# A hybrid decoder trunk on one core: gate rows between the first merge's rounds, the recurrent branch's halves interleaved, the first fox projection ahead of the merge

## The reference, cut to what matters

```python
def causal_depthwise_conv(x, w, b):           # 4 taps
    y = xp[:, 0:S] * w[0] + b
    for k in range(1, CONV_WIDTH):
        y = y + xp[:, k:k + S] * w[k]
...
def rg_lru(x, wa, ba, wx, bx, lam):           # x: the convolved input, 8 blocks of 128 channels
    r = sigmoid(blockdiag(x, wa) + ba)
    i = sigmoid(blockdiag(x, wx) + bx)
    log_a = -LRU_C * r * softplus(-lam)
    a, u = exp(log_a), sqrt(-expm1(2 * log_a)) * (i * x)
    h[t] = a[t] * h[t-1] + u[t]
...
# forgetting attention ("fox", 16 heads of 64) and mLSTM (8 heads of 128)
c = cumsum(log_sigmoid(f_logit))              # the gate rows: one row of 512 tokens for each head
merged = sum_b sigmoid(gate_b) * (y_b @ w_br_b)
x = x + merged @ w_out
x = x + PEER(rms_norm(x))                     # product-key experts
```

## Time and profile before

| | |
|---|---|
| median of 3 runs | 4959.5 us (4953.31 to 4968.77) |
| the profiled execution | 4969.86 us, span 4968.0 us |
| mean granted clock of PE | 0.954 |
| PE, DVE, ACT, POOL busy | 90%, 64%, 36%, 55% |
| layer 1, first full slot to the first fox step | 38.5 to 297.7 us |
| the same place in layer 2 | some 2475 us later |

### The profile page before, as it was taken

How to read it: one execution, slowest core, us unless ns; L and a number is a source line. 1 busy time by engine, 2 the same in 40 slices (tenths; PEclk the granted TensorE clock), 3 DMA queues, 4 the chain that set the end, 5 groups by cost and what they waited for, 6 DMA issues and landing times.

```text
span 4968.0 us, 73244 instructions
## 1 busy us (share of the span) xinstructions
PE 4472.6 (90%) x21194; PEld 3701.0 (74%) x21194; DVE 3170.9 (64%) x5031; ACT 1764.3 (36%) x3196; POOL 2725.2 (55%) x1477
## 2 busy tenths in 40 slices
PE   6899999889988887999978999998898888879998
PEld 4666775679888886777756667756798888867776
DVE  7434224448889775888884342243488897768888
ACT  2234213114555652333322341231145556523332
POOL 5643663555455665555456426636554566645554
PEclk8999999999999998999989999999999999989999
DMA  2211221124578999999712112212246799999996
GB/s 96 68 60 35 76 81 46 68 71 133 180 242 257 297 294 309 342 336 331 288 67 72 56 35 81 80 44 69 71 141 185 240 259 297 301 313 341 348 333 248
DMA packets 463132, 893.19 MB, mean 180 GB/s; under 512 B 41376, under 2 KB 320416, under 8 KB 459808
## 3 DMA queue, kind: packets, MB, share of 16 engines
q1 hardware_dynamic: 387424, 617.22, 38.3%
q0 software_dynamic: 73728, 268.47, 15.7%
q10 hardware_dynamic: 1728, 4.89, 0.3%
HBM read 787.65 MB, written 102.76 MB: 179 GB/s over the span
## 4 chain that ended last, share of the span: by engine, by line
PE 59%; DVE 16%; DMA 10%; issue 8%; ACT 4%; SPq 2%; DVEq 1%; POOL 1%; ACTq 0%; another core or an unknown queue 0%; POOLq 0%
DMA ring<-v_tab 6%; PE pair L749 6%; PE bank L749 6%; PE bank L1120 5%; PE bank L1125 5%; PE bank L1115 4%; PE bank L1063 4%; PE bank L775 3%; DMA ring<-u_tab 3%; PE pair L775 3%; PE pair L752 3%; PE bank L752 3%; PE bank L906 2%; PE bank L1094 2%; PE bank L1067 2%
## 5 line engine op out<-in xcount | busy, mean ns | idle before, releaser
L631 POOL TENSOR_TENSOR w_hi<-ring,ones 128x1024 fp32r<-128x1024 f32 x272 | 546.4, 2009 | 939.0 <-PE bank L775 276.5
L619 POOL TENSOR_TENSOR w_lo<-ring,w_hi 128x1024 fp32r<-128x1024 f32 x256 | 633.2, 2474 | 566.5 <-ACT w_hi L1408 559.7
L1063 PE MATMUL bank<-xT,w_hi 128*128 128x384 f32 x2048 | 729.8, 356 | 22.6 <-ACT gst L1420 18.9
L1063 PE MATMUL bank<-xl_peer,w_hi 128*128 128x384 f32 x2048 | 707.0, 345 | 0.4 <-issue 0.4
L634 POOL TENSOR_TENSOR w_lo<-ring,w_hi 128x1024 fp32r<-128x1024 f32 x272 | 690.1, 2537 | 21.3
L1414 ACT CAST w_hi<-ring 128x1024 fp32r<-128x1024 f32 x256 | 269.6, 1053 | 716.3 <-PE bank L1125 442.1
L1408 ACT CAST w_hi<-ring 128x1024 fp32r<-128x1024 f32 x256 | 268.9, 1050 | 650.5 <-DVE ring L1976 510.2
L2068 DVE TENSOR_TENSOR cl<-att,ch 128x384 fp32r<-128x384 f32 x256 | 354.9, 1386 | 212.0 <-ACT ch L1479 205.0
L625 POOL TENSOR_TENSOR w_lo<-ring,w_hi 128x1024 fp32r<-128x1024 f32 x128 | 306.6, 2395 | 310.2 <-ACT w_hi L1414 310.2
L1115 PE MATMUL bank<-w_hi,ch 128*128 128x512 f32 x1536 | 395.9, 393 | 48.3 <-ACT ch L1479 48.2
L1063 PEld LDWEIGHTS bank<-xT,w_hi 128*128 128x128 f32 x2048 | 404.3, 197 | 26.5 <-ACT w_hi L1408 16.5
(11 more groups left out here) (321 smaller groups left out, 9268.3 us busy)
## 6 DMA issues: line engine op xcount, KB each, us to landing
ring<-v_tab SPq DMA_DIRECT2D x256, 512.0 KB
ring<-w_stream SPq DMA_DIRECT2D x240, 512.0 KB
ring<-u_tab SPq DMA_DIRECT2D x512, 128.0 KB
g_spill<-gst SPq DMA_DIRECT2D x256, 192.0 KB
hn<-u_tab SPq DMA_DIRECT2D x256, 128.0 KB
x_last<-u_tab SPq DMA_DIRECT2D x256, 128.0 KB
w_spill<-vg SPq DMA_DIRECT2D x12, 2048.0 KB
w_spill<-att SPq DMA_DIRECT2D x12, 2048.0 KB
```

Source lines behind the costliest of these rows:

```text
L619: nc.gpsimd.tensor_tensor(w_lo[s % 2][:, :], ring[2 + s % 2][:, :], w_hi[s % 2][:, :].bitcast(F32), ALU.subtract)\
L631: nc.gpsimd.tensor_tensor(w_hi[b][:, 0:n], src, ones[:, 0:1].to_broadcast([P, n]), ALU.mult)\
L1063: nc.tensor.matmul(out, w_hi[s % 2][:, c * P:(c + 1) * P], dense_parts(c)[part], start=(c == 0 and part == 0), stop=False)
```

## The change

1. The rounds are now LRU 2, FV 2, FZ 1, MA 4, FQ 3: the first fox projection, formerly FQ 0, is a round FZ of its own ahead of the merge. SP's loads, POOL's splits and `forget_rows(0)`, PE's projection and ACT's four copies move with it. The fox tile of even rounds lies in another place, since `qk` is the recurrent branch's TH.
2. The gate rows: at the head DVE only takes them from bank 4 (f_row, i_row). The rest is a generator that yields after each step or two. One step runs ahead of merge round 0, then 10, 10 and 5 pieces after rounds 0, 1 and 2. COLS follows the merge.
3. The recurrent branch: the first tap is an Identity activation with scale and bias on ACT (`first_tap`). DVE's order is conv(0), decay(0), conv(1), recur(0), decay(1), lru_low(0), recur(1), lru_low(1), where decay holds L1683 and L1692, recur L1695 to L1703, and lru_low is half of L1710.
4. PE's order: LRU 0, two slots of LRU 1, `gate_products(0)`, two slots of LRU 1, FV 0, half of `gate_products(1)`, three slots of FV 1, the other half, the fourth slot, FZ, MA, COLS, fox steps.

```diff
-ROUNDS = dict(LRU=2, FV=2, MA=4, FQ=4, MV=2, ...
+ROUNDS = dict(LRU=2, FV=2, FZ=1, MA=4, FQ=3, MV=2, ...
...
 # PE
+                for s in range(4):
+                    project(L, "LRU", 0, s, x_parts(xl_mix))
+                for s in range(2):
+                    project(L, "LRU", 1, s, x_parts(xl_mix))
                 gate_products(0)
+                for s in range(2, 4):
+                    project(L, "LRU", 1, s, x_parts(xl_mix))
                 project_tokens(L, "FV", 0, of_tile(xT), xl_of_tile)
-                gate_products(1)
+                gate_products(1, range(2))
+                values = tokens_beside(L, "FV", 1, of_tile(xT), xl_of_tile, 24)
+                for _ in range(3):
+                    next(values)
+                gate_products(1, range(2, 4))
+                next(values)
+                values.close()
+                for s in range(4):
+                    project(L, "FZ", 0, s, x_parts(xl_mix))
+                merge(L, "MA", y_hi_lru, ("LRU", 0, 2))
...
 # ACT
+                def first_tap(i, s):
+                    k = 4 * i + s
+                    act.wait_ge(drained_sem[s], drnd(L, "LRU", i) + 2)
+                    nc.scalar.activation(xc[:, s, :], xpad[:, k, 0:SEQ], ACT.Identity, scale=pcol("conv_w", k),
+                                         bias=pcol("conv_b", k)).then_inc(tap_ready.sem, 1)
...
+                for s in range(4):
+                    conv_input(0, s)
+                    first_tap(0, s)
+                conv_input(1, 0)
+                conv_input(1, 1)
+                lru_gates(0, range(4))
+                act.dma_start(lruw, ...).then_inc(lruw_ready, 16)
+                conv_input(1, 2)
+                conv_input(1, 3)
+                act.wait_ge(xc_free.sem, xc_free.at(L, "LRU", 0, 1))
+                for s in range(4):
+                    first_tap(1, s)
+                decay_exp(0)
+                decay_root(0)
+                values(L, "FV", 0)
+                act.wait_ge(lru_done.sem, lru_done.at(L, "LRU", 1, 0))
+                lru_gates(1, range(2))
+                lru_high(L, 0)
+                lru_gates(1, range(2, 4))
+                decay_exp(1)
+                values(L, "FV", 1)
+                decay_root(1)
+                for s in range(4):
+                    fox_query_key(0, s)
+                lru_high(L, 1)
+                for j in range(2):
+                    gate(L, "MA", 0, 0, j)
+                exponential("G", rows[:, 1, :])
+                merge_gates(L, "MA", 0, 1)
...
 # DVE
+                with dve.Fori(0, 1):
+                    conv(0)
+                    decay(0)
+                    conv(1)
+                    recur(0)
+                    decay(1)
+                    lru_low(0)
+                    recur(1)
+                    lru_low(1)
...
+                row_work = gate_sums()
+                for i, pieces in enumerate((10, 10, 5)):
+                    if i == 0:
+                        next(row_work)
+                    merge_round(L, "MA", i)
+                    for _ in range(pieces):
+                        next(row_work, None)
+                for _ in row_work:
+                    pass
+                merge_round(L, "MA", 3)
```

More of the change, by code:

```diff
@@ L847, in _, with gate_products @@
                          x_parts(xl_mix), lambda: low_wait(L, "N1")).then_inc(filled[4].sem, 1)
[L850 to L854, removed]
+                def gate_products(i, slots=range(4)):
                     pe.wait_ge(lruw_ready, 32 * L + (16 * i + 16))
-                    for s in range(4):
+                    for s in slots:
                         pe.wait_ge(conv_done.sem, conv_done.at(L, "LRU", i, s + 1))
@@ L936, in _ @@
                 project_tokens(L, "MV", 1, of_tile(xT), xl_of_tile)
-                merge(L, "MB", y_hi, ("FQ", 3))
+                merge(L, "MB", y_hi, ("FQ", 3, 1))
                 with pe.Fori(0, 2) as i:
@@ L1030, in _ @@
                     beside.close()
-                merge(L, "MC", y_hi, ("MQ", 3), 1)
+                merge(L, "MC", y_hi, ("MQ", 3, 1), 1)
                 stand(pe)
@@ L1192, in _, with exponential, fox_query_key, conv_input @@
                 act.dma_start(nwb[:, :], nrows[2 * L + 1].partition_broadcast(P)).then_inc(nw_loaded, 16)
-                for ph in ("P", "G"):
+                def exponential(ph, tile):
                     act.wait_ge(zexp_in.sem, zexp_in.at(L, ph, 0, 1))
-                    tile = lp[:, 0, :] if ph == "P" else rows[:, 1, :]
                     nc.scalar.activation(tile, tile, ACT.Exp).then_inc(zexp_out.sem, 1)
[L1198 to L1207, removed]
+                exponential("P", lp[:, 0, :])
+                def fox_query_key(i, s):
+                    proj_wait(L, *fox_round(i), s)
+                    nc.scalar.activation(fox_qk[i % 2][:, s, :], bank[s][:, :], ACT.Copy,
+                                         scale=FOX_D ** -0.5 if s % 2 == 0 else 1.0)\
+                        .then_inc(drained_sem[s], 1)
+                def conv_input(i, s):
+                    proj_wait(L, "LRU", i, s)
+                    nc.scalar.copy(xpad[:, 4 * i + s, CONV - 1:], bank[s][:, :]).then_inc(drained_sem[s], 1)
+                def first_tap(i, s):
[3 more added lines that the diff above has]
+                                         bias=pcol("conv_b", k)).then_inc(tap_ready.sem, 1)
+                def lru_gates(i, slots):
+                    for s in slots:
                         for g in range(2):
@@ L1632, in _ @@
-                c.wait()
-                c.step(V.scalar_tensor_tensor(out=rows[:, 0, :], in0=rows[:, 4, :], scalar=-2.0, in1=rows[:, 0, :],
-                                              op0=ALU.mult, op1=ALU.add))
-                c.wait()
-                c.step(V.tensor_tensor_scan(cum[:, :], ones[0:NROW, 0:1].to_broadcast([NROW, SEQ]), rows[:, 0, :], 0.0, ALU.mult, ALU.add))
-                c.wait()
-                dve.wait_ge(drained_sem[4], drained[4].at(L, "G", 0, 1))
-                c.step(V.tensor_tensor(g_row[:, :], rows[0:ML_H, 5, :], cum[0:ML_H, :], ALU.subtract))
```

245 lines of the change are left out of this document (138 added, 107 removed).

## The result

The changed kernel takes 4887.2 us (median of 4 runs, 4884.95 to 4899.56), the kernel before, measured beside it, 4964.1: a ratio of 0.9852 [0.9826, 0.9878]. A second measurement gave 4893.1 and 0.9857 [0.9835, 0.9880]. The forecast was 4922.5, its range 4900 to 4944: the sign was right, the gain, some 77 us, is twice the 37 that I gave.

What follows compares the result with a forecast made beforehand. TensorE, busy 4472.6 of 4968.0 us, was taken as the bound, winnable only where idle or slow-clocked; layer 1's steps gave 19.7 us, less 1.2, 18.5; two layers 37, from 4959.5 to 4922.5 us, range 4900 to 4944.

Steps and rivals of the forecast that it cites:

- (a): Gate rows moved between merge rounds: charged nothing, since merge steps up to 4, then 8 us late stay within 16.3 us.
- (f): Sixteen merge slots, 87.0 us, plus 0.5 for moved transposes: fox steps start at 278 instead of 297.7.
- (b): First half's convolution, first tap on ACT: TensorE idles 6 us instead of 13.5 before the first gate product, at 79.3.
- rival 3: POOL runs dry whenever TensorE waits, speeding DVE; second convolution 1.7 us a step, gain 27 a layer, 4905 us; chance 0.18.
- rival 2: TensorE becomes split-bound as DVE's long steps and scans delay splits: gain 1 to 3 a layer, 4955 us; chance 0.07.
- (c): Second half's convolution, 2.2 us a step: ACT's values copies wait behind decay_root(0), TensorE idles 9.5 us until 134.6.
- (d): FV round 1: three slots and cold start to 152.6, four products to 156.3, fourth slot to 161.7.
- (e): Moved fox projection: 21.8 us plus 6.3 for late splits and cold clock, ending 189.8; y_lo ready at 196.7.
- the 1.8 us for a cold slot: Charge of 1.8 us for TensorE's slower clock after each stall of 2 us or more.
- rival 4: Slower: second half's y_lo comes after 221, holding the merge; at 232 a layer loses 11, 4982 us; chance 0.07.
- Rivals 1: Every DVE step from the second convolution to y_lo waits a whole split: gain 12 a layer, 4936 us; chance 0.19.

## Why the prediction was wrong, by its own steps

**The term that was not in it.** Every step, from (a) to (f), was about the head, and the rest of the kernel was taken to come later by the same amount. It did not: the experts, whose code isn't edited, gained 25 us in the profile. Padding alone brings 25 us (ratio 0.9949) and takes back 20 (0.9892 against 0.9852). The prediction asked of SP's queue only whether its loads come in time, not where its loops would lie. Of the 33 us by which the profiled gain of 70.3 exceeds the 37, it is 25; the head's surplus is 10, and the mixers took 2 back. The kernel before held the sign of it: pauses of SP called "issue" at L523 in the chain of waits, which I didn't read in that stretch.

**(b), mis-sized.** The first product was to start at 79.3 behind 6 us of idle time, and started at 75.26 behind 2.75. I gave the six steps that release it 15.2 us (63.8 to 79), 2.5 each, between 2.2 and a full turn; they took 12.1 (63.13 to 75.26), 2.0 each, below my lower end. One of the six took 0.74 us and the first 1.12, the others 2.3 to 2.9. POOL's timeline shows the room:

```profile
67.25 2.22 POOL L643 TENSOR_TENSOR w_hi<-ring,ones 128x1024 fp32r<-128x1024 f32 x1 [0.75 <-PE bank L764]
69.54 2.72 POOL L646 TENSOR_TENSOR w_lo<-ring,w_hi 128x1024 fp32r<-128x1024 f32 x1
72.69 1.89 POOL L643 TENSOR_TENSOR w_hi<-ring,ones 128x1024 fp32r<-128x1024 f32 x1 [0.43 <-PE bank L764]
```

It waits 0.4 to 0.8 us for a free buffer between two slots, and a step of DVE fits in there without a turn. Once POOL has no buffer left (behind 77.3), the last steps go at 1.3 (three from 75.26 to 79.20). That is the mechanism of my rival 3, but only behind the first product; the earlier start comes from turns that were not paid. The head gained 22 to 25 us a layer, between my 18.5 and rival 3's 27, without the 1.7 us steps that rival 3 wants of half 1.

The kernel before had the step's price without any turn, in its convolution beside the starving TensorE:

```profile
91.06 2.74 DVE L1671 SCALAR_TENSOR_TENSOR big<-att,pv,big 128x512 f32<-128x512 f32 x4 [0.20 <-DVE big L1668]
```

That is 0.69 us each. The 0.55 us of (b) and rival 2 for a short DVE operation stands in no row; being lower, it isn't what made the forecast late.

**(c), right in size and place, its cause only in part.** 2.19 us a step against 2.2; the stall 8.88 against 9.5, at the place, by the instruction and behind the root that the step names. It was carried 5 us earlier by (b). But what sets its length is DVE's chain with its turns, and not ACT's queue: with the values ahead of the root the wait only changed its place. The taps early show what the stall was made of, DVE's idle 9.25 us behind ACT's last input copy.

**(d), right.** The fox projection starts at 157.65 against 161.7: the 4 to 5 us already won, kept.

**(e), nearly right.** 26.1 us (157.65 to 183.75) against 28.1. One split took over 4 us, as forecast, and two more 3.9, beside DVE's long steps, and four slots waited between 0.2 and 1.4 us. This POOL row has the longest:

```profile
159.20 4.32 POOL L646 TENSOR_TENSOR w_lo<-ring,w_hi 128x1024 fp32r<-128x1024 f32 x1
```

The clock in 153:186 stayed at 1.00; the 1.8 us for a cold slot was not paid. y_lo was ready at 191.0, not 196.7; with the merge also earlier its cover is 4.3 us, where I had 4, and rival 4, the slower case by y_lo, was far off. Moved behind the merge, the projection leaves 15.50 us of idle time, so its place is worth 11 to 15 us a layer.

**(a) and (f), right.** The merge takes 89.15 us against 88.2 with all the gate rows in it. The merge step behind six of them came late (the row at 231.29) and cost no bank. The windows of the kernel after, columns as in the earlier trace rows, show TensorE unbroken beside the gate rows (207:262), and the lower clock in the stall's window (122:136) alone. The same view gives 0.81 for 75.26:84.10, behind the wait of 2.75 us; from 134 to the fox steps it is 1.00:

```profile
122.00:136.00 14.00, 6.31 (x20) 5.09 (x21) 11.96 (x8) 3.84 (x5) 0.14 (x1) 0.63 0.00 0
153.00:186.00 33.00, 29.20 (x124) 22.55 (x123) 29.64 (x9) 12.52 (x13) 28.49 (x10) 1.00 0.24 79
207.00:262.00 55.00, 54.93 (x242) 44.97 (x242) 53.31 (x29) 3.90 (x6) 46.97 (x21) 1.00 0.29 95
```

The fox steps start at 272.90 instead of 278: 24.8 us earlier than before, of which 18.5 was forecast. (b) accounts for 4, (e) for 2, and the 1.2 that I took off for stalls too short for the table was not needed; the merge takes 1 back. Rivals 1 (turns paid in full) and 2 (TensorE bound by splits) are excluded by the same rows.

**The tap's cost, right for the wrong reason to care.** No table load stands between L1239 and L1255 in ACT's timeline, as the Trainium skill says of Identity (ScalarE: Activation LUTs, Table sets: the hidden batching unit). It takes 0.82 us, not the copy's 0.59. But it bought nothing that the runs can tell.

**What stays open.** The unedited mixers took from 736 to 751 us in these profiles, with a granted clock of 0.95 in the slowest (272.90:1024.29 of the kernel after) and 0.97 in the fastest (285.05:1021.29 with the gate rows at the head). Time and clock go together; I didn't find what sets the clock. For the same reason the totals of the kernels with the values first and with the tap on DVE, 4878.5 and 4874.2, aren't explained: their heads are those of the changed kernel, they ran on another chip than its second measurement, and their ratios lie 0.3 to 0.5% below its own. No run takes the two halves' interleaving away alone, so its part in the head's 22 to 25 us isn't shown, and the part of the gate rows is known only together with the held copies.

## What to carry to other kernels

Adding instructions to a queue moves every loop behind them: before a gain or loss is put down to an edit, cut the span at instructions both kernels have, look at the stages that no edit touches, and try the same number of idle instructions in the kernel before. When two engines take turns, a step's price belongs to what the other does at that moment, so a stall of the consumer partly pays for itself, and removing it can cost the producer as much; a chain of short steps beside splits doesn't pay every turn in full (2.0 and 2.2 us a step here, 0.7 without turns). When an experiment moves work back, look which waits move with it. To move the wait of an engine, ask what its producer waited for: reordering the queue that ends the stall did nothing, starting the producer 7 us earlier (89.12 against 96.38) won 8 to 11 us a layer.

## What the runs showed of the hardware that was not expected

- SP stands for 4.3 to 6.9 us at the jump back of a loop of 272 instructions and for 2.2 to 4.7 just behind it, or not at all, depending on where the loop lies: 184 and 186 fetches in an execution with the pauses, 136 to 138 without. The windows of the experts of layer 1, before, show the DMA engines 80% busy (the last column but one), which leaves little room to make up for loads issued late (argued, not tested). The pauses cost 20 to 25 us in all:

```profile
1046.64:2493.14 1446.50, 1303.68 (x6698) 1169.82 (x6698) 1152.20 (x1960) 615.06 (x1053) 798.82 (x478) 0.96 0.80 263
```

- One DVE operation with two inputs, of 24x512 or 8x512 elements, takes 0.68 us with POOL idle and 2.1 to 2.8 beside splits; a 128x2048 one goes from 2.29 to 4.37, and four scans of 128x512 from 4.57 to 12.02. POOL's w_lo goes from 2.40 to 4.32 us beside the latter.
